# Decoder layer on 8 cores: x normed per token chunk, stick-breaking as a product scan with DMA transposes, a ones column in V, weights cast by DMA

## The reference, cut to what matters

```
u = RMSNorm(x);  proj = u @ w_in      # q,k,v of 8 stick-breaking heads, q,k,v of 8 forgetting heads, forget logits, two gates
# stick-breaking head (dh = 128), strictly causal, s < t
z = q k^T / sqrt(128)
w[t,s] = sigmoid(z[t,s]) * prod_{s<j<t} (1 - sigmoid(z[t,j]))      # the reference does it in log space
o_sb = w @ v
# forgetting head, s <= t, c = running sum of log sigmoid(f_logit + b_forget)
p = softmax(z[t,s] + c[t] - c[s]);  o_fx = p @ v
merged = sigmoid(g_sb) * (o_sb @ w_branch_sb) + sigmoid(g_fx) * (o_fx @ w_branch_fox)
h = x + RMSNorm(merged @ w_out);  out = h + RMSNorm(swiglu(RMSNorm(h)))      # ff width 5632
```

## Time and profile before

| | us |
|---|---|
| runs shown: two | 4626.53 and 4863.05, median 4744.79 |
| profiled execution, its slowest core's span | 4605.1 (cores 4578.5 to 4605.1) |
| the nearer of the two runs beside that span | 4626.53, so 21.4 around the span |
| TensorE busy | 4013.2 (87%) |
| VectorE / ScalarE / GpSimd busy | 1442.7 / 1151.3 / 582.9 |

### The profile page before, as it was taken

The page is one execution under the profiler, slowest core; times in us unless marked ns, Lnnn a source line. Parts: engine busy times, 40 slices in busy tenths (PEclk is TensorE's granted clock), DMA queues, the critical chain, the costliest instruction groups (busy, mean ns, idle before and its releaser), DMA issues.

```text
span 4605.1 us, 55119 instructions; the slowest of 8 cores (4578.5 to 4605.1 us)
## 1 busy us (share of the span) xinstructions
PE 4013.2 (87%) x18692; PEld 1797.5 (39%) x18692; DVE 1442.7 (31%) x1718; ACT 1151.3 (25%) x1995; POOL 582.9 (13%) x772
## 2 busy tenths in 40 slices
PE   2588888899998799979977599998999999998973
PEld 0233333344443344434433244443444444443431
DVE  1433333343443333123322323222222223223332
ACT  3067767733334011211123111111111000000100
POOL 0022122100101111001123000010000100000013
PEclk5799999999999899989999799999999999999986
DMA  7410121121210544654468655554664666658997
GB/s 232 147 34 34 34 62 34 34 63 34 63 35 9 184 148 145 199 168 154 156 183 265 215 191 188 196 196 153 226 206 160 194 199 191 193 170 285 311 275 227
DMA packets 165124, 712.96 MB, mean 155 GB/s; under 512 B 18928, under 2 KB 27632, under 8 KB 103408
## 3 DMA queue, kind: packets, MB, share of 16 engines
q1 hardware_dynamic: 136176, 642.31, 44.3%
q10 hardware_dynamic: 18432, 33.56, 2.0%
q0 software_dynamic: 10240, 33.56, 1.9%
HBM read 633.86 MB, written 75.50 MB: 154 GB/s over the span
## 4 chain that ended last, share of the span: by engine, by line
PE 77%; DMA 12%; DVE 3%; ACT 3%; issue 3%; POOL 1%; SPq 0%; DVEq 0%; ACTq 0%; POOLq 0%
PE ps L78 77%; DMA wstD_174_216<-wfd_t 4%; DMA xs_25_67<-xT 2%; DMA mh_99_141<-mixs 1%; DMA hs<-hst_101_143 1%; DVE rec_93 L78 1%; ACT W_46_88 L78 1%; DMA wst_17_59<-wqkv_t 1%; DMA wstA_57_99<-wg_t 0%; DMA outT<-ot_194_236 0%; DVE uT_50 L78 0%; POOL hst_101_143 L78 0%; ACT sq_27_69 L78 0%; ACT W_45_87 L78 0%; DMA wstA_83_125<-wg_t 0%
## 5 line engine op out<-in xcount | busy, mean ns | idle before, releaser
L78 PE MATMUL ps<-u_117_159,wgu_0_139_181 128*128 128x512 bf16 x704 | 161.1, 382 | 48.2 <-DVE wgu_0_139_181 L78 48.2
L78 PE MATMUL ps<-aT_160,wd_175_217 128*128 128x512 bf16 x704 | 162.3, 392 | 37.0 <-DVE wd_175_217 L78 37.0
L78 PE MATMUL ps<-uT_50,wbf_1_19_61 128*128 128x512 bf16 x512 | 123.0, 388 | 81.0 <-DVE wbf_1_19_61 L78 77.4
L78 PE MATMUL ps<-aT_160,wd_176_218 128*128 128x512 bf16 x704 | 163.6, 394 | 22.3 <-DVE wd_176_218 L78 22.3
L78 PE MATMUL ps<-aT_160,wd_150_192 128*128 128x512 bf16 x704 | 155.8, 381 | 15.6 <-DVE wd_150_192 L78 15.6
L78 PE MATMUL ps<-u_117_159,wgu_0_166_208 128*128 128x512 bf16 x704 | 160.6, 382 | 3.0 <-DVE wgu_0_166_208 L78 3.0
L78 PE MATMUL ps<-u_117_159,wgu_0_141_183 128*128 128x512 bf16 x704 | 159.1, 379 | 0.0
L78 PE MATMUL ps<-u_117_159,wgu_1_140_182 128*128 128x512 bf16 x704 | 159.1, 379 | 0.0
L78 PE MATMUL ps<-u_117_159,wgu_1_142_184 128*128 128x512 bf16 x704 | 159.1, 379 | 0.0
L78 PE MATMUL ps<-u_117_159,wgu_1_167_209 128*128 128x512 bf16 x704 | 159.1, 379 | 0.0
L78 PE MATMUL ps<-u_117_159,wgu_0_168_210 128*128 128x512 bf16 x704 | 159.1, 379 | 0.0
(11 more groups left out here) (383 smaller groups left out, 6620.2 us busy)
## 6 DMA issues: line engine op xcount, KB each, us to landing
wstD_172_214<-wfd_t SPq DMA_DIRECT2D x32, 1024.0 KB, 8.4
wstD_173_215<-wfd_t SPq DMA_DIRECT2D x32, 1024.0 KB, 8.7
wstD_174_216<-wfd_t SPq DMA_DIRECT2D x32, 768.0 KB, 9.4
xs_24_66<-xT SPq DMA_DIRECT2D x16, 1024.0 KB, 5.5
xs_25_67<-xT SPq DMA_DIRECT2D x16, 1024.0 KB, 5.7
wst_15_57<-wqkv_t SPq DMA_DIRECT2D x16, 1024.0 KB, 7.2
wst_16_58<-wqkv_t SPq DMA_DIRECT2D x16, 1024.0 KB, 10.0
wst_17_59<-wqkv_t SPq DMA_DIRECT2D x16, 1024.0 KB, 12.4
```

What stands on the lines that cost most here:

```text
L78: ins = getattr(eng, meth)(**kw)
```

## The change

- **x.** The host adds a copy of x, `xq`, in 4 token chunks. x is loaded once, in 16 pieces of 1 MB with 6 buffers; per chunk of 512 tokens: 4 squares, 16 matmuls of ones, 1/rms, 16 VectorE operations into `uT`, and then head 0's projection of that chunk, evicted by ScalarE. `uT` has one dependency per chunk (`uR`).
- **Weights.** Loaded and cast to bf16 by the DMA itself, issued from GpSimd, straight into `wbf`; no `wst`, no VectorE casts.
- **Projection.** v is made untransposed: `uT` blocks are the stationary operand and the v weights move, 256 matmuls of 128 columns, each with its own weight load, no transposes. 24 items per head. For stick-breaking heads q and k are evicted by ScalarE and v by VectorE, else all by VectorE.
- **stage2** becomes three filler items in head 5.
- **Stick-breaking.** 16 steps per head, one per query block of 128, the keys 0 to n = 128(qb+1) along the free dimension. The mask is added by a matmul with the identity. ScalarE: sigmoid(-z) to fp32 and sigmoid(z) to bf16, up to 1024 wide. VectorE: a running product (`tensor_tensor_scan`) over n reversed keys, and one multiply over n. SP: a DMA transpose of `[128, n]`. TensorE: per key block one matmul of 128 columns with V, three steps later (`LAG`). `Filler.tick` goes by the step's size.
- **Forgetting.** P is the stationary operand and V with a ones column moves (129 columns), so the denominator comes in the same matmul; the diagonal mask is a matmul; the reciprocals are 4 of 128x1 per chunk, and a DMA transpose turns the chunk's output.
- PSUM is allocated as four pairs of banks.

```diff
+    def turn(self, Q, ds, out, in_, reads=(), writes=()):
+        return self.dma_multi(Q, ds, [(out, in_)], reads, writes, "dma_start_transpose")
...
+    def load_head(hh, ws, after=()):
+        br, h = divmod(hh, NH)
+        for j in (1, 2, 0):
+            dst = wbf[ws][j]
+            kb.dma(POOL, dst.ds, dst.t[:, :, :], wqkv_t[br * 24 + j * 8 + h], reads=list(after), writes=[dst.r])
...
+                    kb.group(PE, [("matmul", dict(out=bt[:, j * 128:(j + 1) * 128], lhsT=uT.t[:, k, t0:t0 + 128],
+                                                  rhs=wv.t[:, k, :], start=(k == 0), stop=(k == KC - 1)))
+                                  for k in range(KC)],
+                             reads=[wv.r, uR[tc]], writes=[br_])
...
+    load_x(6)
+    kb.dma(POOL, wfb.ds, wfb.t[:, :, :], wf_t, writes=[wfb.r])
+    load_head(heads[0], 0, after=[xs[3].r])
+    for tc in range(NCH):
+        norm_x(tc)
+        load_x(4 * tc + 10)
+        if tc == 1:
+            load_head(heads[1], 1, after=[xs[1].r])
+        for it in proj_items(0, 0, (ACT, ACT, ACT), [tc]):
+            it()
...
+    def sb_A(g, par, qb):
+        qT, kT, V = qkv[par]
+        n = (qb + 1) * 128
+        b_, k_, i_, w_, wt = be[g % 2], ke[g % 2], In[g % 2], Wb[g % 2], WT[g % 4]
+        for lo in range(0, n, 1024):
...
+            kb.group(PE, calls, reads=[qT.r, kT.r, cbf.r], writes=[zr[0], zr[1]])
+            kb.op(ACT, "activation", dict(out=k_.t[:, lo:hi], in_=zt[:, 0:hi - lo], func=AF.Sigmoid, scale=-1.0),
+                  writes=[zr[0], zr[1], k_.r])
+            kb.op(ACT, "activation", dict(out=b_.t[:, lo:hi], in_=zt[:, 0:hi - lo], func=AF.Sigmoid),
+                  writes=[zr[0], zr[1], b_.r])
+        kr = k_.t[:, 0:n][:, ::-1]
+        kb.op(DVE, "tensor_tensor_scan", dict(out=i_.t[:, 1:n + 1][:, ::-1], data0=kr, data1=kr, initial=1.0,
+                                              op0=ALU.mult, op1=ALU.bypass), reads=[k_.r], writes=[i_.r])
+        kb.op(DVE, "tensor_tensor", dict(out=w_.t[:, 0:n], in0=b_.t[:, 0:n], in1=i_.t[:, 2:n + 2], op=ALU.mult),
+              reads=[b_.r, i_.r], writes=[w_.r])
+        kb.turn(SP, wt.ds, wt.t[:, 0:qb + 1, :], w_.t[:, 0:n], reads=[w_.r], writes=[wt.r])
+
+    def sb_B(g, hh, par, qb):
...
+        kb.group(PE, [("matmul", dict(out=bO[:, j * 128:(j + 1) * 128], lhsT=V.t[:, b, 0:128], rhs=wt.t[:, b, :],
+                                      start=(b == 0), stop=(b == qb))) for b in range(qb + 1)],
+                 reads=[V.r, wt.r], writes=[rO])
...
+        for j in range(max(0, b - 4 * c), 4):
+            at, ar = acc(c, j)
+            calls.append(("matmul", dict(out=at, lhsT=p.t[:, j * 128:(j + 1) * 128], rhs=V.t[:, b, 0:129],
+                                         start=(b == 0 and j % 2 == 0), stop=(b == 4 * c + j), skip_group_check=True)))
...
+        for qb in range(NB):
+            todo, later[:] = list(later), []
+            sb_A(g, i % 2, qb)
+            for f in todo:
+                f()
+            fl.tick(qb + 1)
+            pendB.append((g, hh, i % 2, qb))
+            if len(pendB) > LAG:
+                sb_B(*pendB.pop(0))
+            g += 1
+        fl.flush()
```

More of the change, by code:

```diff
@@ L198, with __init__, tick @@
 class Filler:
[L199 removed]
+    def __init__(self, items, total):
         self.items = list(items)
[L201 to L210, removed]
+        self.n = len(self.items)
+        self.total = max(1.0, float(total))
+        self.done = 0.0
+        self.out = 0
+    def tick(self, w=1.0):
+        self.done += w
+        want = min(self.n, int(self.n * self.done / self.total + 1e-6))
+        while self.out < want:
+            self.items[self.out]()
+            self.out += 1
     def burst(self, k):
[L213 to L215 removed]
+        while k > 0 and self.out < self.n:
+            self.items[self.out]()
+            self.out += 1
+            k -= 1
     def flush(self):
[L218 to L219 removed]
+        self.burst(self.n)
 class Slot:
@@ L708, in _emit @@
-    if dbg is not None and "OT" in dbg:
-        ds = kb.dsem("dbgOT")
-        allr = [OT_res[hh][c] for hh in heads for c in range(NCH)]
-        for hh in heads:
-            ev = kb.dma(SP, ds, dbg["OT"][hh], OTs[hh], reads=allr)
-        final_events.append(ev)
+        v_ = Slot(kb, f"V{par}", [128, NB, 130], BF16)
+        qkv.append((q_, k_, v_))
+        kb.op(POOL, "memset", dict(ap=v_.t[:, :, 128:130], constant=1.0), writes=[v_.r])
+    pb = [banks[0], banks[1]]
+    cnt = {"p": 0, "z": 0, "o": 0}
@@ new lines, in _emit @@
+    pendB = []
+    g = 0
+    for i in range(NH):
+        hh = heads[i]
+        nx = (i + 1) % 2
+        items = proj_items(nx, nx, (ACT, ACT, DVE) if i + 1 < NH else (DVE, DVE, DVE))
+        if i == 5:
+            items = stage2_items() + items
+        load_head(heads[i + 2], i % 2)
+        fl = Filler(items, 136)
+        for qb in range(NB):
[9 more added lines that the diff above has]
+        fl.flush()
@@ new lines, in _emit @@
+    while pendB:
+        sb_B(*pendB.pop(0))
+    seq = [(hh, c, b) for hh in heads[NH:] for c in range(NCH) for b in range(4 * c + 4)]
+    fl = None
+    fx_A(0, seq[0][0], seq[0][0] % 2, 0, 0)
+    fx_A(1, seq[1][0], seq[1][0] % 2, seq[1][1], seq[1][2])
+    fx_act(0, *seq[0])
+    for g, (hh, c, b) in enumerate(seq):
+        if c == 0 and b == 0:
+            if fl is not None:
+                fl.flush()
+            if hh + 1 < 2 * NH:
+                nx = (hh + 1) % 2
+                fl = Filler(proj_items(nx, nx, (DVE, DVE, DVE)), 40)
+                if hh + 2 < 2 * NH:
+                    load_head(hh + 2, hh % 2)
+            else:
+                fl = Filler([], 1)
+        last_of_head = c == NCH - 1 and b == 4 * c + 1
+        if last_of_head:
+            fl.flush()
+        if g + 1 < len(seq):
+            fx_act(g + 1, *seq[g + 1])
+        fx_B(g, hh, hh % 2, c, b)
+        if g + 2 < len(seq):
+            h2, c2, b2 = seq[g + 2]
+            fx_A(g + 2, h2, h2 % 2, c2, b2)
+        fl.tick()
@@ L714, in _emit @@
+    while later:
+        later.pop(0)()
     al.release(m_w)
```

593 lines of the change are left out of this document (238 added, 355 removed).

## The result

Two runs of the changed kernel took 4335.6 and 4306.9 us, median **4321.3 us**, against 4744.8. In some executions of either kernel the cores of one die show a lower granted clock and take longer (by its length the 4863 us in the median before is taken for one); ratios and means from here on leave these out, and a time without an interval had too few others for one. So counted the ratio is 0.931 [0.914, 0.949]: faster. The profile is that of the 4335.6 us execution; its slowest core is core 6, span 4334.1 us, so 1.5 us lie around the span.

The account below looks back on a forecast made before the run. TensorE, busy 87% of the span, was taken as the bound. From 4605 us, prologue -45, stick-breaking -166, forgetting heads -89 and last head -5 gave 4300, with 21.4 around the span 4320 us; range 4250 to 4540.

Parts of the forecast that it names:

- Prologue: Work ahead of the heads: chunks follow one another at 39 us each, 170 us against 215.5, a gain of 45.
- TensorE's prices: Matmul costs per head: 0.216 us for 512 columns, 0.057 for 128; 58.2 us a head, 60 at the granted clock.
- rival 3: Weight loads don't hide: 392 narrow matmuls per head at 0.098 instead of 0.057 us; 4580 us, chance 0.05.
- The scan: VectorE in stick-breaking heads: 20 us a head taken, hidden; VectorE would pass TensorE's 60 us from 2.6 ns per column.
- Transposes: DMA transposes of stick-breaking weights: near the plain load rate, 30 us per head, hidden.
- rivals 1 and 2: Stick-breaking DMA transposes at the packets' price, 4505 us, chance 0.13; or block by block, 4929 us, chance 0.12.
- stand behind nothing: Weight loads issued from GpSimd: 3 MB per head have some 60 us to land, the slowest of three takes 12.4.
- the stall of 4 us per head: After a stick-breaking head's last step, TensorE waits for transposes, as the smallest steps give about 10 us for three.
- the stage2 term: Stage2 within the stick-breaking stage: 6.7 us of matmuls and waits, 8 us in all.
- The evictions' allowance: Stick-breaking heads: projection banks wait for evictions behind a scan, 3 us per head allowed.
- Forgetting heads: Seven heads at 60 + 1.5 us, without the 3.8 us wait for q's eviction: 430 against 519 us, a gain of 89.
- The 21.4 us around the span: Time outside the profiled span, added to the forecast span of 4300 us to give 4320.

## Why the prediction was right, and where it was not

- **Prologue, right.** 168.3 us against 170, and the order of the chunks is the one described (the norm moved ahead took 45 us away).
- **TensorE's prices, right.** 58.2 us a head and 6.7 for stage2 are 472 us, at the clock of 0.97 486 us; on core 1 without loads, at 0.97, TensorE is busy 486.7. The 32 narrow matmuls of a piece of v take 1.95 us, 57 ns each, so rival 3 fell.
- **The scan, right in the conclusion.** 4427 ns for 2048 columns and 2284 for 1024 are 2.09 ns per column, 39 us a head, against 20 taken: the nearest kind of operation was no guide to its size. The bounds held it and so did the condition (2.6 ns). The page "DVE: opcode table, instruction layouts, handler registers and perf-mode slots" (Datapath and trigger behaviour) of the Trainium skill says half throughput, which at the 0.96 GHz of the prediction is an estimate of 2.08 ns: the trace agrees, 2.09 ns.
- **Transposes, the side right.** 0.021 us per packet, not the 0.080 of queue 10, so 17,408 packets over 16 engines are 23 us a head: rivals 1 and 2 fell, for as long as the transposes are alone. The Trainium skill's 261 GB/s ("DMA: Bandwidth & Descriptors", Latency and other measured facts), which stands there for a non-contiguous middle dimension and gives an estimate of 17 us, is somewhat fast beside this row.
- **The step that failed** is the sentence that the 3 MB of weights per head, issued from GpSimd, "stand behind nothing", with the stall of 4 us per head that was reckoned without them. I asked whether the weights would be in time, and they were. I didn't ask what they do to the others: issued at the turn, because there the buffer is released, they take the DMA engines from two wide transposes for which TensorE has no cover just then. The stall was 81 us on the slowest core instead of 32. With the loads out, or in twelve pieces, the mean of the cores is 25 or 36 us instead of 60, and the most on any core 34 or 44 instead of 81; at the turns between heads that is 2 to 6 us, the size of the forecast's 4. So the failed term is 81 - 32 = 49 of the 66 us.
- **The other 17 us.** By the windows and the waits of core 6: TensorE busy 495 us against 487; stage2's waits 12 against the 1 that its term of 8 us leaves beside 6.7 of matmuls; evictions 13 against 24; the rest, the two ends of the stretch among it, 14 against 5. So the stage2 term was too small by 11 us: its matmuls were priced, the queue that its small VectorE operations fill was not. The evictions' allowance was too large by as much, which is luck.
- **What V costs was not asked.** The 3 us a head for evictions behind a scan were twice what came (8.7 us for V, 2.4 for kT and 1.5 for qT, 12.6 of 24), but only since V is no longer turned by TensorE. By the prices V's two forms are 13.8 + 0.9 and 14.6 us, a draw; on the chip the kernel with the old form is 92 us slower, some 60 of it in the stages that V's form touches, or 225 with the transposes right behind the product.
- **Forgetting heads, right but small by 13 us.** 59.6 us a head against 61.5: the evictions' stall of 1.5 us isn't there, and the granted clock was 1.00 in this stage. The 3.8 us waits for q went as forecast, but not by the reciprocal alone, since they stay away when it comes back. The last head gave 15 instead of 5 us, which no run took apart.
- **The 21.4 us around the span** were two executions, not one: in the executions since, of either kernel, time and slowest core lie 1 to 2 us apart. A median should have been set beside the span, not an overhead added.

So the total was right with two errors of 66 and about 50 us in it; without the luck it would have been near 4386, inside the range all the same.

## What to carry to other kernels

When an edit moves data movement from an engine to DMA, list what else is issued in the same microseconds, and look at the stage's boundary, where the release of buffers sends the big loads just as the small tiles give TensorE no cover; spread such loads over the stage. When long instructions, or many small ones in a row, are put on an engine, TensorE's work that depends on that engine within one step can pay their length, so price the queue and not only the operation, and change the data's layout until little depends on it. And read the cores of one profile against each other: where they wait differently, their spans give the price of the wait without a run. That holds for one order of work: the four-step lag, the loads in mid-head and the work at the turn each raised the 523 us.

## What the runs showed of the hardware that was not expected

- A transposing packet of 256 bytes shows 0.021 us alone and 0.102 us, waiting included, beside casting loads; the landing goes from 3.2 to 21 us, at worst 32.2. Whether the cast, GpSimd's queue or the bytes alone do it was not tested.
- A transpose of up to sixteen 128x128 blocks shows 1.3 us (median; at most 2.2 on core 1 of the run without loads) on SP's queue and lands in 3.3 us (median, least 2.2): blocks of one instruction do not follow one another at 1.3 us each.
- The cores of one execution wait between 43 and 81 us for the same transposes in the same program; in another execution it is core 2 and not core 6 that waits longest.
- Beside pauses the granted clock was lower: with waits of up to 14.7 us spread over the heads it was 0.84 instead of 0.93 on core 0, and the matmuls' own time rose by 62 us. That the pauses are the cause isn't shown: cores 2 and 3 of the run without loads had 0.82 with no more waiting than their neighbours.
